# Second mixer's attention by pairs of heads instead of unit by unit, beside the dense matmuls of a two-block network

## The chip, the cores and the metric

One core of one Trainium2 chip runs the whole program. The metric is device time in microseconds (us) of one execution. The engines are TensorE (PE; its weight loads are listed as PEld), VectorE (DVE), ScalarE (ACT), GpSimd (POOL) and SyncE (SP, which issues the weight loads from memory). Each runs its own list of instructions in order and waits on semaphores.

## The reference, cut to what matters

Two network blocks run one after the other on 256 tokens of width 1024. The second has a feed-forward part, a mixer, and another feed-forward part. The mixer has two branches: a windowed attention (8 query heads of width 64 on 2 key/value heads, 16 meta tokens, a per-head distance bias, a sink logit) and a gated linear attention (4 heads). Each branch is multiplied by a weight matrix and a sigmoid gate, and the sum goes through w_out.

```python
s_band = jnp.einsum('bcqkgd,bcskd->bkgcqs', qf, kb).astype(jnp.float32) * scale
s_band = s_band - slopes[None, :, :, None, None, None] * dist[None, None, None]
s_meta = jnp.einsum('bcqkgd,bmkd->bkgcqm', qf, km).astype(jnp.float32) * scale
p = jax.nn.softmax(jnp.concatenate([s_meta, s_band, s_sink], axis=-1), axis=-1).astype(v.dtype)
of = (jnp.einsum('bkgcqm,bmkd->bcqkgd', p[..., :N_META], vm)
      + jnp.einsum('bkgcqs,bcskd->bcqkgd', p[..., N_META:N_META + NB], vb))
```

## The kernel before, in words

**Dense products.** Every float32 weight matrix is split on the chip into an upper part (ScalarE, `split`, L600, tile `hi`) and a lower part (DVE, `split`, L1128, tile `lo`), and every product is three matmuls: upper by upper, upper by lower, lower by upper (L1962 to L1964). Weights come through a ring of four slots (`raw`, `hi`, `lo`). A slot's weights feed one `half` of 24 matmuls of 256 columns. Results go to four accumulator banks `acc` in PSUM, two of them per pair of output tiles; `acc_free` says that a pair of banks has been read. Four more banks, `wk`, serve everything else.

**The stage.** The mixer's projections are the phase `in2k`. Its gates are `in2g`, 16 halves, of which four are done before the attention begins. `brb` (linear branch, four parts) and `bra` (attention branch, four parts) are the branch matrices, `wout2` is w_out. The attention (PE, L2608 to L2655) is laid between twelve halves of `in2g` and the four parts of `brb`, all listed by hand on each engine.

**A unit** is one head and one block of 128 queries: `UNITS` (L353) runs over head pairs `hp`, blocks `b` and the head `par` of the pair, 16 units. An early block (b = 0) sees 16 meta keys and 128 others (144 columns), a late one (b = 1) 272. The head of the pair sits in the upper or lower 64 partitions of `qT2`. Per step u, TensorE does:
- the scores of unit u (L2616), in bank u % 2, after the maximum of unit u - 1,
- for unit u - 2: a wait for its normalised probabilities, and their transposes by key tile into bank 2 (L2628, L2630),
- one dense piece of 24 matmuls,
- a wait for the transposes' copy, and the values (`transposed_out`, L2400) in bank 3. Here the value matrix `avz2` holds zeros on both sides of the 64 value columns, so a matmul of 128 columns adds one head's output to the one half of the partitions and zeros to the other; both heads of a pair accumulate in one group.

DVE has per step: the softmax sum and normalisation of unit u - 1 (`softmax_sum`, L1408 to L1410), the maximum with the bias added (L1878), the head pair's lower part (`heads_lower`, L1415), the lower part of a weight slot (`gates_split`), the evacuation of two gate tiles times the inverse norm (`gates_evac`, L1829), the output of a linear head (L1894 to L1897: reciprocal, product with the gain, product with the gate) in four of the steps, its lower part (L1902), and later `branch_out` (L1864), which reads a part of `brb` out of its bank. At the end come four products of gate and branch (L1912). ScalarE has per step: the copy of the transposes (L1066, L1067), the exponential and the sink's exponential (L766, L767), the upper part of a weight slot, the copy of a head pair (`heads_out`, L774), the copy of a linear head (L1080), and two sigmoids (L1058). GpSimd builds the bias of each head in a double buffer (L579).

**After it**, `evac_bra` on DVE (L1920, L1922, L1926) multiplies each part of `bra` by its gate, adds, and makes the lower part; ScalarE copies the upper part (L1089) and then splits the next weights. `wout2` starts when the third part has been read out of its bank.

**The first mixer** (L2187 to L2219) does its attention by pairs: `scores` puts two heads on two row halves, `values_out` two heads on two column halves.

```python
if 1 <= u <= 12:
    gates_half(u + 3)
elif 13 <= u <= 16:
    ...
    branch_part("brb", 4, u - 13)
elif u == 17:
    pe.wait_ge(ol_ready, 7)
    branch_part("bra", 0, 0, range(3))
```

Of the kernel before, what the change touches and what calls it, by code (L numbers as in the profile page):

```python
# [6 lines left out]
F32 = mybir.dt.float32  # L7
# [7 lines left out]
P = 128  # L15
# [97 lines left out]
def program(nc, dr, out):  # L113
    with ExitStack() as root:
# [146 lines left out]
        avz2 = sbuf(blk2, "avz2", [P, 3, 2, 192])  # L261
# [91 lines left out]
        UNITS = [(hp, b, par) for hp in range(4) for b in range(2) for par in range(2)]  # L353
# [124 lines left out]
        def _(pool):  # L478
# [93 lines left out]
            pool.memset(avz2[:], 0.0)  # L572
# [12 lines left out]
        def _(act):  # L585
# [183 lines left out]
            def heads_out(n, hp):  # L769

                if n == 0:
                    act.wait_ge(half_done, 4)
                act.wait_ge(o_ps, n + 1)
                act.activation(mixH[:, hp, :], wk[:, 3 if n >= 4 else 2, 0:T], ACT.Copy).then_inc(oh_ready, 1)  # L774
# [210 lines left out]
            def attention_keys():  # L985

                act.wait_ge(zero2, 1)
                act.wait_ge(av2_ps, 1)
                act.activation(avz2[0:META, 0, :, 64:128], wk[0:META, 2, 0:P].rearrange("p (g d) -> p g d", g=2), ACT.Copy)
                act.activation(avz2[:, 1:3, :, 64:128], wk[:, 2, P:3 * P].rearrange("p (t g d) -> p t g d", t=2, g=2),  # L990
# [70 lines left out]
            for u in range(18):  # L1061
                w = u - 2
                if w >= 0:
                    b = UNITS[w][1]
                    act.wait_ge(pt_ps, 16 + w + 1)
                    act.activation(pT2[0:META, w % 2, 0:P], wk[0:META, 2, 0:P], ACT.Copy)  # L1066
                    act.activation(pT2[:, w % 2, P:P * (b + 2)], wk[:, 2, P:P * (b + 2)], ACT.Copy).then_inc(pt_ready, 1)  # L1067
                if u < 16:
                    hp, b, par = UNITS[u]
                    nk = META + P * (b + 1)  # L1070
                    exp_scores(16 + u, Sm2[:, u % 2, 0:nk], sinkn[:, 8 + 2 * hp + par:9 + 2 * hp + par])

                gates_split(u + 6)
                if w >= 0 and w % 4 == 3:
                    heads_out(4 + w // 4, w // 4)
                if u in (3, 5, 7, 9):

                    n = u // 2 - 1
                    act.wait_ge(yb_ready, n + 1)
                    act.activation(mixH[:, 4 + HEADS[n], :], og[:, n, 0:T], ACT.Copy).then_inc(ybh_ready, 1)  # L1080
                if u == 16:
                    sigmoid(1)
            sigmoid(0)

# [1626 lines left out]
```

## Time and profile before

| | us |
|---|---|
| timed runs, median of 3 | 1023.13 (1020.88 to 1025.48) |
| the profiled execution's own time | 1014.95 |
| its span | 1013.2 |
| TensorE busy, share of the span | 977.3, 96% |
| DVE busy | 657.0, 65% |
| ScalarE busy | 498.4, 49% |
| GpSimd busy | 75.4, 7% |
| mean granted TensorE clock | 0.988 |

In the lines of the timeline the first number is an instruction's start, the second its duration (or that of a merged group of x instructions, from the first start to the last end), and in brackets stands the idle time of the engine before it, with what ended it. Durations on one engine overlap: a matmul is recorded for 0.28 us where the next one starts 0.12 after it. What an instruction takes of its engine's time is the distance of two starts. A float32 matmul shows as two records.

### The profile page before, as it was taken

How to read it: one execution, taken by the hardware profiler on the slowest of the kernel's cores; microseconds unless marked ns; L12 is line 12 of the kernel's file. 1: busy time of each engine (PE TensorE's matmuls, PEld its weight loads, DVE VectorE, ACT ScalarE, POOL GpSimd, SP SyncE). 2: the span in 40 equal slices, each digit the busy share in tenths (PEclk: the TensorE clock that was granted, in tenths of full speed). 3: DMA queues.
4: the chain of work that ended last, by engine and by line, in shares of the span. 5: the costliest groups of instructions: out<-in, count | busy, mean ns of one | idle time of the engine just before them, and what ended most of it. 6: DMA issues, size and time to landing. Idle time of an engine off the chain costs nothing.

```text
span 1013.2 us, 19459 instructions
## 1 busy us (share of the span) xinstructions
PE 977.3 (96%) x7547; PEld 910.4 (90%) x7547; DVE 657.0 (65%) x1008; ACT 498.4 (49%) x774; POOL 75.4 (7%) x101
## 2 busy tenths in 40 slices
PE   4998999999999999999999999999999999999996
PEld 2776777989999999899999999998888999999995
DVE  4788887577666765765555555754966775565553
ACT  3664546654545543554445334644545555444530
POOL 0102012110000021000000012000210100000000
PEclk8999998999999999999999999999999999999998
DMA  9953346456656794165556736542433556666841
GB/s 349 385 175 126 116 134 215 144 173 189 194 168 189 194 299 152 62 214 175 166 176 189 219 104 196 167 144 64 125 109 121 169 166 207 187 184 199 218 122 41
DMA packets 189439, 175.41 MB, mean 173 GB/s; under 512 B 7344, under 2 KB 178624, under 8 KB 189008
## 3 DMA queue, kind: packets, MB, share of 16 engines
q1 hardware_dynamic: 183888, 154.29, 49.8%
q0 software_dynamic: 4928, 17.51, 5.0%
q10 hardware_dynamic: 576, 2.97, 0.7%
q8 instruction: 31, 0.51, 0.2%
q14 instruction: 16, 0.13, 0.0%
HBM read 173.67 MB, written 1.05 MB: 172 GB/s over the span
## 4 chain that ended last, share of the span: by engine, by line
PE 86%; DVE 8%; ACT 3%; issue 2%; DMA 1%; SPq 0%; DVEq 0%; ACTq 0%
PE acc L1962 22%; PE acc L1963 22%; PE acc L1964 22%; PE acc L2348 2%; DVE lo L1128 2%; PE wk L2400 1%; PE acc L2152 1%; DMA slab_hi<-in_w_ada 1%; PE acc L2153 1%; PE acc L2154 1%; ACT hi L600 1%; DVE inv L1182 1%; PE wk L2616 1%; PE wk L1962 1%; PE wk L1964 1%
## 5 line engine op out<-in xcount | busy, mean ns | idle before, releaser
L1128 DVE TENSOR_TENSOR lo<-raw,hi 128x1024 fp32r<-128x1024 f32 (+1 forms) x260 | 333.7, 1296 | 199.9 <-ACT hi L600 199.5
L600 ACT ACTIVATE hi<-raw 128x1024 fp32r<-128x1024 f32 (+1 forms) x260 | 282.9, 1098 | 132.2 <-PE acc L1964 123.7
L1962 PE MATMUL acc<-nH,hi 128*128 128x272 f32 (+3 forms) x1016 | 291.2, 287 | 2.9 <-DVE gab L1920 1.1
L1963 PE MATMUL acc<-nL,hi 128*128 128x272 f32 (+3 forms) x1016 | 289.7, 285 | 0.0
L1964 PE MATMUL acc<-nH,lo 128*128 128x272 f32 (+3 forms) x1016 | 288.7, 284 | 0.0
L1962 PEld LDWEIGHTS acc<-nH,hi 128*128 128x128 f32 (+1 forms) x1016 | 191.4, 188 | 5.4 <-DVE lo L1128 2.1
L1963 PEld LDWEIGHTS acc<-nL,hi 128*128 128x128 f32 (+1 forms) x1016 | 191.0, 188 | 0.4
L1964 PEld LDWEIGHTS acc<-nH,lo 128*128 128x128 f32 (+1 forms) x1016 | 190.9, 188 | 0.2
L1962 PE MATMUL acc<-gH,hi 128*128 128x256 f32 (+1 forms) x528 | 149.5, 283 | 0.8 <-DVE lo L1128 0.8
L1964 PE MATMUL acc<-gH,lo 128*128 128x256 f32 (+1 forms) x528 | 149.2, 283 | 0.0
L1963 PE MATMUL acc<-gL,hi 128*128 128x256 f32 (+1 forms) x528 | 149.0, 282 | 0.0
L1962 PE MATMUL acc<-mixH,hi 128*128 128x256 f32 x400 | 113.9, 285 | 0.9 <-DVE mixL L1415 0.9
L1963 PE MATMUL acc<-mixL,hi 128*128 128x256 f32 x400 | 113.2, 283 | 0.0
L1964 PE MATMUL acc<-mixH,lo 128*128 128x256 f32 x400 | 113.1, 283 | 0.0
L1962 PEld LDWEIGHTS acc<-gH,hi 128*128 128x128 f32 x528 | 99.1, 188 | 1.0 <-DVE lo L1128 1.0
L1963 PEld LDWEIGHTS acc<-gL,hi 128*128 128x128 f32 x528 | 99.6, 189 | 0.0
L1964 PEld LDWEIGHTS acc<-gH,lo 128*128 128x128 f32 x528 | 99.2, 188 | 0.0
L1962 PEld LDWEIGHTS acc<-mixH,hi 128*128 128x128 f32 x400 | 76.7, 192 | 1.1 <-DVE mixL L1415 1.1
L1963 PEld LDWEIGHTS acc<-mixL,hi 128*128 128x128 f32 x400 | 76.8, 192 | 0.0
L1964 PEld LDWEIGHTS acc<-mixH,lo 128*128 128x128 f32 x400 | 76.7, 192 | 0.0
L544 POOL TENSOR_TENSOR sq<-sq 128x256 f32<-128x256 f32 (+1 forms) x28 | 24.5, 876 | 497.4 <-ACT sq L890 442.5
L890 ACT ACTIVATE sq<-R (+3 forms) x36 | 15.8, 440 | 57.8 <-DVE R L1702 49.7
(421 smaller groups left out, 1307.9 us busy)
## 6 DMA issues: line engine op xcount, KB each, us to landing
raw<-in_w_in SPq DMA_DIRECT2D x52, 512.0 KB, 3.6
raw<-in_w_ffn_in SPq DMA_DIRECT2D x44, 512.0 KB, 4.4
raw<-in_ffn_w_gate SPq DMA_DIRECT2D x44, 512.0 KB, 3.6
raw<-in_ffn_w_up SPq DMA_DIRECT2D x44, 512.0 KB, 3.6
raw<-in_ffn_w_down SPq DMA_DIRECT2D x32, 704.0 KB, 4.8
stage<-in_w_ada POOLq DMA_DIRECT2D x24, 512.0 KB, 5.5
raw<-in_w_ffn_out SPq DMA_DIRECT2D x16, 704.0 KB, 6.5
raw<-in_w_out SPq DMA_DIRECT2D x16, 512.0 KB, 3.4
```

Of the source, the lines that this page charges most:

```text
L544: ins = pool.tensor_tensor(sq[:, 0, 0:width], sq[:, 0, 0:width], sq[:, k, 0:width], ALU.add)
L600: act.activation(hi[:, j, 0:width], raw[:, j, 0:width], ACT.Copy).then_inc(hi_ready, 1)
L890: act.activation(sq[:, k, 0:width], R[:, k, t0:t0 + width], ACT.Square).then_inc(sq_ready, 1)
L1128: dve.tensor_tensor(lo[:, j, 0:width], raw[:, j, 0:width], hi[:, j, 0:width].bitcast(F32), ALU.subtract).then_inc(lo_ready, 1)
L1182: link(dve.reciprocal(inv[:, 0:width], rms[:, 0:width]))
L1962: pe.matmul(out_, wH, xH, start=start, stop=False)
L1963: pe.matmul(out_, wH, xL, start=False, stop=False)
L1964: return pe.matmul(out_, wL, xH, start=False, stop=stop)
L2152: pe.matmul(out_, n5H[:, k, rows], hi[:, k // 2, w], start=k == 0, stop=False)
L2153: pe.matmul(out_, n5H[:, k, rows], lo[:, k // 2, w], start=False, stop=False)
L2154: return pe.matmul(out_, n5L[:, k, rows], hi[:, k // 2, w], start=False, stop=k == KD - 1)
L2348: ins = pe.matmul(out_, ws[:, j, w], xs[:, k, :], start=k == 0 and m == 0 and n == 0, stop=k == KD - 1 and n == 2, skip_group_check=True)
```

## The change

The step by units becomes a loop over eight pairs n (head pair n // 2, block n % 2), on each of the three engines.

- TensorE, per pair: both heads' scores one after the other on the two row halves, in banks 0 and 1; the values of the pair before, on two column halves, from `av2`, which holds the 128 value columns without zeros; a dense piece; the transposes of both heads, into the banks that held their scores; a second dense piece. The first values wait for the linear heads' root means. After the loop: the last values, three quarters of `bra`'s first part, a wait for the last heads' lower part, and the rest.
- Head pairs alternate between banks 2 and 3 (`head_bank`).
- ScalarE, per pair: two exponentials, the heads' copy (n = 2, 4, 6), a split, one copy of both heads' transposes (two instructions of twice the width), a split, a linear head's copy (n = 0, 1, 3, 4). Then: sigmoid, the last heads' copy, split 22, sigmoid, split 23.
- DVE, per pair: two maxima, two softmax sums, heads' lower part, a split, a gate evacuation, a linear head's output (n = 0, 1, 3, 4), a split, a linear lower part (n = 1, 2, 4, 5); brb's parts are read out in pairs 6 and 7. Then: the last heads' lower part, split 22, the last part of brb, the four products, split 23.
- GpSimd no longer clears the value matrix, and ScalarE doesn't wait for it.

```diff
-        avz2 = sbuf(blk2, "avz2", [P, 3, 2, 192])
+        av2 = sbuf(blk2, "av2", [P, 3, P])
...
+        LINEAR_AT = {0: 0, 1: 1, 3: 2, 4: 3}
+        def head_bank(n):
+            return wk[:, 2 + n % 2 if n >= 4 else 2 + n // 4, 0:T]
...
-            pool.memset(avz2[:], 0.0)
...
+            for n in range(8):
+                hp, b = divmod(n, 2)
+                for par in range(2):
+                    exp_scores(16 + 2 * n + par, Sm2[:, par, 0:keys_to(b)], sinkn[:, 8 + 2 * hp + par:9 + 2 * hp + par])
+                if n >= 2 and b == 0:
+                    heads_out(4 + hp - 1, hp - 1)
+                gates_split(6 + 2 * n)
+                act.wait_ge(pt_ps, 16 + 2 * n + 2)
+                act.activation(pT2[0:META, :, 0:P], wk[0:META, 0:2, 0:P], ACT.Copy)
+                act.activation(pT2[:, :, P:P * (b + 2)], wk[:, 0:2, P:P * (b + 2)], ACT.Copy).then_inc(pt_ready, 2)
+                gates_split(7 + 2 * n)
+                if n in LINEAR_AT:
+                    i = LINEAR_AT[n]
+                    act.wait_ge(yb_ready, i + 1)
+                    act.activation(mixH[:, 4 + HEADS[i], :], og[:, i, 0:T], ACT.Copy).then_inc(ybh_ready, 1)
+            sigmoid(1)
+            heads_out(7, 3)
+            gates_split(22)
             sigmoid(0)
+            gates_split(23)
...
+            for n in range(8):
+                hp, b = divmod(n, 2)
+                shifted_maxima(n)
+                for par in range(2):
+                    softmax_sum(16 + 2 * n + par, Sm2[:, par, 0:keys_to(b)])
+                if n >= 2 and b == 0:
+                    heads_lower(4 + hp - 1, hp - 1)
+                if n == 7:
+                    branch_out(1)
+                gates_split(6 + 2 * n)
+                if n <= 6:
+                    gates_evac(n + 1)
+                if n in LINEAR_AT:
+                    linear_out(LINEAR_AT[n])
+                gates_split(7 + 2 * n)
+                if n - 1 in LINEAR_AT:
+                    linear_lower(LINEAR_AT[n - 1])
+                if n == 6:
+                    branch_out(0)
+                if n == 7:
+                    branch_out(2)
+            heads_lower(7, 3)
+            gates_split(22)
+            branch_out(3)
+            dve.wait_ge(gates_ready, 1)
+            dve.wait_ge(acc_free[1], USE["brb"] + 2)
+            for j in range(4):
+                b = gab[:, KD + 2 * j:KD + 2 * j + 2, :]
+                dve.tensor_tensor(b, b, branch[j], ALU.mult)
+            gates_split(23)
...
+            def paired_values(n):
+                hp, b = divmod(n, 2)
+                pe.wait_ge(pt_ready, 16 + 2 * n + 2)
+                if n == 0:
+                    pe.wait_ge(grms, 2)
+                if b == 0 and hp >= 2:
+                    pe.wait_ge(ol_ready, 4 + hp - 1)
+                g4 = hp // 2
+                for t in range(b + 2):
+                    rows = slice(0, META if t == 0 else P)
+                    for par in range(2):
+                        ins = pe.matmul(wk[HD * par:HD * par + HD, 2 + hp % 2, P * b:P * b + P],
+                                        av2[rows, t, HD * g4:HD * g4 + HD], pT2[rows, par, P * t:P * t + P],
+                                        start=t == 0, stop=t == b + 1)
+                if b == 1:
+                    ins.then_inc(o_ps, 1)
...
+            for n in range(8):
+                paired_scores(n)
+                if n >= 1:
+                    paired_values(n - 1)
+                mixer_piece(2 * n)
+                paired_probabilities(n)
+                mixer_piece(2 * n + 1)
+            paired_values(7)
+            pe.wait_ge(ol_ready, 7)
+            branch_part("bra", 0, 0, range(3))
```

`paired_scores(n)` waits for the copy of pair n - 1's transposes, then issues the two score matmuls. `paired_probabilities(n)` waits for each head's normalised probabilities before its transposes. `mixer_piece(i)` is a half of `in2g` for i < 12 and a part of `brb` after that, as before.

## Rows read from the trace of the kernel before

**Rows 1.** The page, section 4: the chain that ended last, by engine.
```profile
PE 86%; DVE 8%; ACT 3%; issue 2%; DMA 1%; SPq 0%; DVEq 0%; ACTq 0%
```

**Rows 2.** Windows: length, busy us (instructions) by engine, granted clock, DMA share, GB/s.
```profile
700.60:789.20 88.60, 86.56 (x633) 76.49 (x633) 66.51 (x142) 49.28 (x115) 13.08 (x6) 1.00 0.35 114
...
710.00:715.00 5.00, 5.00 (x40) 4.48 (x39) 4.83 (x15) 2.73 (x8) 2.48 (x1) 1.00 0.35 104
```

**Rows 3.** Timeline, TensorE: a late block's values, scores, transposes, between dense matmuls.
```profile
716.76 0.28 PE L1964 MATMUL acc<-nH,lo 128*128 128x256 f32 x1
716.97 1.12 PE L2400 MATMUL wk<-pT,avz 16*128 16x128 f32 x6
718.02 0.51 PE L2616 MATMUL wk<-kS,qT 64*128 64x144 f32 x2
718.46 0.28 PE L2628 MATMUL wk<-cst,Sm 128*16 128x128 f32 x1
...
718.91 0.29 PE L1963 MATMUL acc<-nL,hi 128*128 128x256 f32 x1
719.03 0.28 PE L1964 MATMUL acc<-nH,lo 128*128 128x256 f32 x1
```

**Rows 4.** Timeline, TensorE: an early block's values and a late block's scores.
```profile
726.57 0.90 PE L2400 MATMUL wk<-pT,avz 16*128 16x128 f32 x4
727.40 0.72 PE L2616 MATMUL wk<-kS,qT 64*128 64x272 f32 x2
728.05 0.28 PE L2628 MATMUL wk<-cst,Sm 128*16 128x128 f32 x1
```

**Rows 5.** Timeline, TensorE: paired scores and values in the first mixer.
```profile
114.30 0.59 PE L2195 MATMUL wk<-kTs,qT 64*128 64x512 f32 x1
114.30 0.59 PE L2195 MATMUL wk<-kT,qT 64*128 64x512 f32 x1
114.82 1.09 PE L2217 MATMUL wk<-pT,vat 128*64 128x128 f32 x16
115.85 0.50 PE L2152 MATMUL acc<-hi,n5H 128*128 128x512 f32 x1
```

**Rows 6.** Timeline, DVE: linear output, sum, maximum, split, evacuation.
```profile
708.16 1.74 DVE L1894 RECIPROCAL tC<-tC 128x256 f32<-128x256 f32 x1
...
710.81 0.15 DVE L1408 TENSOR_TENSOR rinv<-rsum,esink 128x1 f32<-128x1 f32 x1
...
711.47 0.49 DVE L1878 CUSTOM_DVE_ANT_0 Sm<-wk,bias,sinkn 128x272 f32<-128x272 f32 x1
...
711.89 1.22 DVE L1128 TENSOR_TENSOR lo<-raw,hi 128x1024 fp32r<-128x1024 f32 x1
713.02 0.68 DVE L1829 TENSOR_TENSOR gab<-acc,inv 128x512 f32<-128x512 f32 x1
713.62 0.15 DVE L1408 TENSOR_TENSOR rinv<-rsum,esink 128x1 f32<-128x1 f32 x1
```

**Rows 7.** Timeline, ScalarE: exponential with sink, then the split.
```profile
712.00 0.52 ACT L766 ACTIVATE Sm<-Sm,negm 128x272 f32<-128x272 f32 x1 [1.85 <-DVE negm L1878]
...
712.71 1.04 ACT L600 ACTIVATE hi<-raw 128x1024 fp32r<-128x1024 f32 x1
```

**Rows 8.** Timeline: ScalarE's table load and sigmoid, bra's first evacuation, wout2's first matmul.
```profile
771.62 1.28 ACT L1058 ACT_TABLE_LOAD   x1
...
774.73 0.25 ACT L1066 ACTIVATE pT<-wk 16x128 f32<-16x128 f32 x1
...
779.86 0.69 DVE L1920 TENSOR_TENSOR gab<-gab,acc 128x512 f32<-128x512 f32 x1 [0.32 <-ACT gab L1058]
...
789.20 0.36 PE L1962 MATMUL acc<-nH,hi 128*128 128x256 f32 x1 [1.11 <-DVE gab L1920]
```

**Rows 9.** Timeline, TensorE: transposes in the first mixer after a wait.
```profile
97.53 1.15 PE L2203 MATMUL wk<-cst,Sm 128*128 128x128 f32 x7 [2.91 <-DVE Sm L1436]
```

**Rows 10.** Windows, columns as in rows 2: what follows that wait.
```profile
98.60:102.00 3.40, 3.40 (x10) 2.70 (x9) 3.33 (x10) 0.82 (x2) 0.00 (x0) 0.50 0.00 0
```

More of the change, by code:

```diff
@@ L773, in heads_out @@
                 act.wait_ge(o_ps, n + 1)
[L774 removed]
+                act.activation(mixH[:, hp, :], head_bank(n), ACT.Copy).then_inc(oh_ready, 1)
             def state_weights(h):
@@ L1898, in _, with linear_out @@
-                if u in (4, 6, 8, 10):
-                    n = u // 2 - 2
-                    dve.wait_ge(ybh_ready, n + 1)
-                    dve.tensor_tensor(mixL[:, 4 + HEADS[n], :], og[:, n, 0:T], mixH[:, 4 + HEADS[n], :].bitcast(F32),
-                                      ALU.subtract).then_inc(ybl_ready, 1)
-                if 14 <= u <= 17:
-                    branch_out(u - 14)
-                if u == 17:
-                    dve.wait_ge(gates_ready, 1)
-                    dve.wait_ge(acc_free[1], USE["brb"] + 2)
-                    for j in range(4):
-                        b = gab[:, KD + 2 * j:KD + 2 * j + 2, :]
-                        dve.tensor_tensor(b, b, branch[j], ALU.mult)
+            def linear_out(n):
+                root = (tC, kdT)[n // 2][:, n % 2, 0:T]
+                dve.wait_ge(gr_ready, 2)
+                dve.wait_ge(grms, n // 2 + 1)
+                link(dve.reciprocal(root, root))
+                link(dve.scalar_tensor_tensor(out=og[:, n, 0:T], in0=og[:, n, 0:T], scalar=col(V_GO), in1=root,
+                                              op0=ALU.mult, op1=ALU.mult))
+                dve.tensor_tensor(og[:, n, 0:T], og[:, n, 0:T], grT[:, HEADS[n], :], ALU.mult).then_inc(yb_ready, 1)
@@ L2394, in _ @@
                     ada_turn(3)
-            def transposed_out(par, b, keys):
-                for i, (v, p) in enumerate(keys):
-                    ins = pe.matmul(wk[:, 3, P * b:P * b + P], v, p, start=par == 0 and i == 0,
-                                    stop=par == 1 and i == len(keys) - 1)
-                if b == 1 and par == 1:
-                    ins.then_inc(o_ps, 1)
             PACED = [(k, s) for k in range(6) for s in range(2)] + [(6, 0), (7, 0), (6, 1), (7, 1)]
@@ new lines, in paired_scores, with paired_probabilities @@
+            def paired_scores(n):
+                hp, b = divmod(n, 2)
+                if n >= 1:
+                    pe.wait_ge(pt_ready, 16 + 2 * n)
+                for par in range(2):
+                    h = 2 * hp + par
+                    keys = kvraw2[:, 0, :] if h // 4 == par else kS2
+                    pe.matmul(wk[:, par, 0:keys_to(b)], qT2[lanes(h), hp, P * b:P * b + P], keys[lanes(h), 0:keys_to(b)],
+                              start=True, stop=True).then_inc(s_ps, 1)
+            def paired_probabilities(n):
+                for par in range(2):
+                    pe.wait_ge(p_norm, 16 + 2 * n + par + 1)
+                    ins = pe.transpose(wk[0:META, par, 0:P], Sm2[:, par, 0:META], ident)
+                    for t in range(n % 2 + 1):
+                        ins = pe.transpose(wk[:, par, P + P * t:2 * P + P * t], Sm2[:, par, META + P * t:META + P * t + P], ident)
+                    ins.then_inc(pt_ps, 1)
@@ new lines, in mixer_piece @@
+            def mixer_piece(i):
+                if i < 12:
+                    gates_half(4 + i)
+                else:
+                    if i == 12:
+                        pe.wait_ge(ybl_ready, 4)
+                    branch_part("brb", 4, i - 12)
+            for n in range(8):
+                paired_scores(n)
+                if n >= 1:
+                    paired_values(n - 1)
+                mixer_piece(2 * n)
+                paired_probabilities(n)
+                mixer_piece(2 * n + 1)
```

102 lines of the change are left out of this document (15 added, 87 removed).

## The prediction

> **What bounds the kernel now.** First the page: the chain that ended last is TensorE for 86% [rows 1], so only what shortens TensorE's own sequence, or a wait in it, moves the end. Then the windows over the stretch that the change touches, from the first scores of the second mixer's attention at 700.6 to the first matmul of the phase wout2 at 789.2 [rows 2]: TensorE is busy 86.56 of 88.60 us, so about 2 us of it are waits. VectorE (DVE) is busy 66.51 us there, but 4.83 of 5.00 in a window where the linear heads' output is worked on: it has spare time in total and almost none in the first half. Then TensorE's timeline, read from start to start, since durations overlap.
>
> **What a unit costs now** [rows 3, 4]. Dense matmuls start 0.12 apart. From the last dense one to the values is 0.21, so a change of the array's shape costs 0.09 beyond the pitch. Values of a late block (three key tiles) take 718.02 - 716.97 = 1.05; of an early block (two) 727.40 - 726.57 = 0.83. Scores take 718.46 - 718.02 = 0.44 and 728.05 - 727.40 = 0.65. Three transposes and one dense matmul take 718.91 - 718.46 = 0.45, so three transposes 0.33, two 0.22. A dense piece is 24 matmuls, 2.87.
>
> **The change on TensorE, part by part.**
> *Scores.* Two heads of a pair go out together on different row halves. The first mixer does this already: its two streams start in the same hundredth [rows 5]. So a pair costs one price, 0.44 or 0.65. For 16 units I count 8.7 now (4.4 after): the first two already run together, so 3.9 saved, and the entries fall from 16 x 0.09 to 9 x 0.09, another 0.6; I keep 4.2 for both, since the last two units enter no scores now.
> *Values.* The compact matrix has 64 columns per head and the two heads go side by side. No row of before shows 16 rows by 64 columns. Lower end: the first mixer's 128x64 pairs, 16 records from 114.82 to 115.85 [rows 5], 0.26 per key tile, so 0.52 early and 0.77 late. Upper end: the pair doesn't overlap and costs two units, 1.66 and 2.10. I take 0.68 and 0.90, the lower end plus 0.15 for the shape change between the 16-row and the 128-row tile, because rows 5 have the same two column halves in the same program. That is 15.0 now against 6.3: 8.7 saved.
> The Trainium skill (TensorEngine Tiling, Key Properties) says that changing the tiling mode, not just the tile, drains the engine; it speaks against this change, which has four mode changes per pair, but it gives no price, and by the 0.09 to 0.15 taken here the sum stands.
> *Transposes and dense pieces* keep their number. TensorE's work falls by 12.9 us in all. The bank moves (heads in turn in two banks, transposes in the score banks), the smaller matrix, and the dropped memset and wait on GpSimd cost nothing: the keys are copied while dense matmuls of the projections run.
>
> **What takes part of it back: the order on DVE.** DVE prices [rows 6]: maximum 0.42, softmax sum 0.66, split 1.13, evacuation 0.60, a linear head's output 710.81 - 708.16 = 2.65. ScalarE's exponential with the sink 712.71 - 712.00 = 0.71 [rows 7]. An early block has 144 columns for 272; I estimate its maximum, sum and exponential at 0.35, 0.60 and 0.60. Now a maximum waits for scores issued a whole unit before, and there is always one unit in hand. After, a pair is one serial chain: scores, two maxima, two exponentials, two sums, transposes. From the first maximum to the second sum's end: 0.5 + 2 x 0.71 + 0.1 + 0.75 = 2.8 late, 2.5 early. TensorE covers it with the previous values and one piece, 0.68 + 2.87 = 3.55 or more; enough, if DVE is free when the scores land.
> Between the second sum and the next maxima DVE has split, evacuation, linear output, split, and about 0.3 waiting for ScalarE's split (1.04, begun when DVE's sum of 0.7 begins): 0.3 + 1.13 + 0.60 + 2.65 + 1.13 = 5.8, and 0.35 more for each lower half. Pair 0 to 1: 5.8 + 2.8 + 0.1 = 8.8 from one second sum to the start of the next second transposes, against TensorE's 0.14 to start again after a wait, second transposes 0.22, piece 2.87, entry and scores 0.74, values 0.68, piece 2.87, first transposes 0.33 = 7.9: a wait of 0.9. Pair 1 to 2: 6.1 + 2.5 + 0.1 = 8.7 against 7.9: 0.8. Pair 2 to 3 has no linear output: none. Pair 3 to 4 lives on the lead that DVE gained: none. Pair 4 to 5: 6.5 + 2.8 + 0.1 = 9.4 against 7.8 and some 0.3 of lead: 1.2. Pair 0 starts behind an activation table load: 0.55. In pair 6 the second dense piece (brb's second part) needs the bank freed by DVE's last gate evacuation, which stands behind the sums, a lower half and a split: 0.35 + 0.3 + 1.13 + 0.68 + 0.14 = 2.6 after the second sum, less the lead of 1.2 that the sum has by then and the transposes' 0.44: 1.0. Sum of waits 4.5.
> So the second transposes of the last pair start at 700.6 + 15 pieces 43.0 + entries 0.7 + scores 4.4 + values 5.4 (seven) + transposes 4.2 + waits 4.5 = 762.7.
>
> **The tail.** The end of the stage is now no longer TensorE's. In the bra phase each part goes evacuate, add, ScalarE copy, ScalarE split, DVE split, evacuate; the first evacuation at 779.86 leads to wout2's first matmul at 789.20, 9.34 us [rows 8], and that chain is unchanged. After, the first evacuation comes at the end of this: transposes land 0.5, pair copy out of PSUM 0.9 (twice as wide as now; bounds 0.4 and 0.9, I take the high one), ScalarE split 0.95, table load and sigmoid 774.73 - 771.62 = 3.1 [rows 8], copy of the last heads 0.3 to its start of the next, split 22 1.05; then on DVE, in its new order, split 1.14, last brb evacuation 0.60, four gate products at 0.60 (the 128x512 shape of [rows 6]), split 23 1.14: 5.3. Together 12.1: 774.8. Before, the sigmoid stood a unit earlier and the gate products ran before the last heads. TensorE meanwhile waits for bra's second bank about 1.5 (last brb evacuation at 770.9, behind the last heads' lower half and split 22), and about 1.3 at each of bra's third and fourth parts and at wout2. wout2 then starts at 774.8 + 9.3 = 784.1, against 789.20: **5.1 us gained**. Check: 12.9 less work, 10.2 of waits against 2.3 now.
>
> The profiled execution took 1014.95 (span 1013.2 and 1.75 around it); less 5.1 that is 1009.9. The three timed runs have a median of 1023.13, 8.2 above the profiled one, and spread 4.6. The sum is a difference, so I put it on the median: 1018.0. A measurement of this kernel can tell about 0.5%, 5.1 us, from no change; the forecast sits on that line.
>
> **Rivals.**
> A. *DVE's waits don't show.* If DVE's lead carries it through the linear heads, the 4.5 of waits go and wout2 starts 4.5 earlier: gain 9.6, 1013.5. For: DVE has 22 us idle [rows 2]. Against: 4.83 of 5.00 just where its order is tightest. 0.13.
> B. *Pairs of values don't overlap in the 16-row form,* or not at all. Seven values at the upper end add 7.5 to TensorE before the last transposes, of which half falls into the waits above: gain 1.3, 1021.8. Against: rows 5. 0.08.
> C. *The clock.* After 2.91 us without a matmul [rows 9] the granted clock was 0.50 over 98.6 to 102.0 [rows 10], the 1.2 GHz level, for 3.4 us. The tail after has four waits of 1.3 to 1.5 within 17 us where before has one or two; a stretch at the low level loses up to 1.7 us of dense matmuls, two on end 3.4, part of it inside waits: gain 2 to 3.5, 1020.4. The Trainium skill (TensorE: Matmul & The Clock Gate, What's actually happening) says that the gate follows how busy the engine has been recently, and by that rule this rival would hold. Against: waits of 1.1 at the end of this stage now left the clock at 1.00 [rows 2]. 0.15.
> D. *Slower: ScalarE late for the exponentials.* In its queue the next pair's exponentials stand behind the pair copy, the second split and the linear copy (0.9 + 0.95 + 0.35 = 2.2 after the transposes). I have about 1.4 of slack before the maxima need it. If the transposes' waits push this past zero, every pair is longer by up to 1.4: eight pairs 11.2, slower by 6.1, 1029.2. It decides from 0.64 us per pair. For: ScalarE waits 1.85 now only because DVE is late. Against: it is busy 49 of 89 us [rows 2]. 0.09.
>
> **How the numbers follow.** The forecast case has 0.55; its own spread of 1.5 either way puts half above the 0.5% line. Faster: A and half the forecast, and a little of C, 0.43. Slower by over 0.5%: D, mostly, 0.07. Within: 0.50. Range: forecast, A, C and B, 1013.2 to 1023.4.
>
> **What would show it.** Right: score records in pairs starting together; values of both heads started within 0.01 and 0.7 to 0.9 per pair; DVE's maxima late in pairs 1, 2 and 5 and TensorE waiting there for the softmax sum; waits of over 1 us before bra's second, third and fourth part; wout2 starting some 83.5 us after the first scores. Wrong: values over 1.5 a pair, a clock under 1.00 between 700 and 785, no TensorE waits in the tail, or a stretch over 88 us.

## The result, and the profile after

| | before | after |
|---|---|---|
| median of ten runs, us | 1022.0 (1015.72 to 1025.62) | 1013.85 (1011.02 to 1019.19) |
| profiled execution, us | 1014.95 | 1015.63 |
| its span, us | 1013.2 | 1013.8 |
| TensorE busy in the span | 977.3 (96%) | 975.2 (96%) |

The ratio of the times is 0.9934, interval 0.9909 to 0.9959: faster, by less than 1%, and the forecast's range holds the time, 0.65 us above its lower end. A second measurement of the same two kernels, further down, gives 0.9957, interval 0.9927 to 0.9987.

The two profiled executions alone would say "no change". That is the first thing to take apart. The changed kernel's scores begin at 706.01, before's at 700.6 [rows 2]; wout2 begins at 789.87 against 789.20; from there to the end both take 223.9 to 224.0. So the stretch fell from 88.62 (first scores to wout2's first matmul, by the records) to 83.86, 4.8 us, and the code ahead of it, where the change drops only the clearing of the value matrix and a wait for it, took 5.4 us longer in this one execution. The experiments return to that.

The page's chain by engine, after:

```profile
PE 81%; DVE 11%; ACT 4%; issue 3%; DMA 1%; SPq 0%; DVEq 0%; ACTq 0%
```

TensorE's share fell from 86% [rows 1] and VectorE's (DVE's) rose from 8% to 11%: work went, waits on VectorE came. The windows over the stretch, with the columns of rows 2, and over two pieces before it:

```profile
706.01:789.87 83.86, 76.52 (x634) 67.89 (x633) 66.67 (x142) 46.88 (x99) 9.61 (x6) 1.00 0.38 120
20.00:30.00 10.00, 8.49 (x34) 6.63 (x31) 6.64 (x17) 6.22 (x12) 0.00 (x0) 1.00 1.06 370
680.00:690.00 10.00, 10.00 (x53) 8.38 (x51) 6.53 (x15) 5.03 (x6) 0.00 (x0) 0.83 0.33 105
```

TensorE is busy 76.52 where it was busy 86.56 [rows 2]: 10.0 less. It idles 83.86 - 76.52 = 7.3 where it idled 2.0. That is 10.0 saved and 5.3 given back. The granted clock is 1.00 in the stretch, but 0.83 in the ten microseconds from 680.

TensorE's timeline where the scores of a late pair (272 columns) and the values of the early pair before it stand, then the values of that late pair:

```profile
713.22 0.49 PE L2623 MATMUL wk<-kvraw,qT 64*128 64x272 f32 x1
713.22 0.49 PE L2623 MATMUL wk<-kS,qT 64*128 64x272 f32 x1
...
713.88 0.80 PE L2647 MATMUL wk<-pT,av 16*64 16x128 f32 x8
714.61 0.39 PE L1977 MATMUL acc<-nH,hi 128*128 128x256 f32 x1
714.84 0.28 PE L1978 MATMUL acc<-nL,hi 128*128 128x256 f32 x1
...
722.61 1.02 PE L2647 MATMUL wk<-pT,av 16*64 16x128 f32 x12
...
723.56 0.39 PE L1977 MATMUL acc<-nH,hi 128*128 128x256 f32 x1
```

Scores of the two heads start in the same hundredth, and the pair takes 713.88 - 713.22 = 0.66, what one head took [rows 4]. Values of two heads take 714.61 - 713.88 = 0.73 and 723.56 - 722.61 = 0.95, where one head took 0.83 and 1.05 [rows 3, 4]. Behind the values, the first dense matmul takes 714.84 - 714.61 = 0.23 instead of 0.12. The summary of TensorE's waits between 700 and 800:

```profile
PE acc L1977 <- DVE gab L1935: 3.5, 3, 1.3
PE wk L2630 <- DVE Sm L1413: 2.1, 6, 0.6
PE acc L1977 <- DVE kdT L1867: 1.3, 1, 1.3
PE acc L1977 <- DVE gab L1832: 0.4, 1, 0.4
```

Each line has total, number and longest. The first and third are the tail: bra's banks and wout2 wait for VectorE. The second is the loop: the softmax sums of pairs 0, 1, 2 and 5. The fourth is pair 6, which waits for a gate evacuation. The tail, on ScalarE:

```profile
769.55 1.04 ACT L607 ACTIVATE hi<-raw 128x1024 fp32r<-128x1024 f32 x1
770.61 1.28 ACT L1064 ACT_TABLE_LOAD   x1
771.90 1.92 ACT L1064 ACTIVATE gab<-gab 128x2048 f32<-128x2048 f32 x1
773.72 0.36 ACT L781 ACTIVATE mixH<-wk 128x256 fp32r<-128x256 f32 x1
```

and on VectorE:

```profile
774.12 0.42 DVE L1418 TENSOR_TENSOR mixL<-wk,mixH 128x256 fp32r<-128x256 f32 x1 [1.67 <-ACT mixH L781]
775.06 1.22 DVE L1131 TENSOR_TENSOR lo<-raw,hi 128x1024 fp32r<-128x1024 f32 x1 [0.52 <-ACT hi L607]
776.20 0.68 DVE L1867 COPY kdT<-acc 128x512 f32<-128x512 f32 x1
776.99 0.69 DVE L1926 TENSOR_TENSOR gab<-gab,tA 128x512 f32<-128x512 f32 x1
...
778.81 0.68 DVE L1926 TENSOR_TENSOR gab<-gab,kdT 128x512 f32<-128x512 f32 x1
779.41 1.22 DVE L1131 TENSOR_TENSOR lo<-raw,hi 128x1024 fp32r<-128x1024 f32 x1
780.54 0.68 DVE L1935 TENSOR_TENSOR gab<-gab,acc 128x512 f32<-128x512 f32 x1
```

and on TensorE:

```profile
776.94 0.39 PE L1977 MATMUL acc<-mixH,hi 128*128 128x256 f32 x1 [1.30 <-DVE kdT L1867]
781.28 0.38 PE L1977 MATMUL acc<-mixH,hi 128*128 128x256 f32 x1 [1.21 <-DVE gab L1935]
785.47 0.39 PE L1977 MATMUL acc<-mixH,hi 128*128 128x256 f32 x1 [1.07 <-DVE gab L1935]
789.87 0.36 PE L1977 MATMUL acc<-nH,hi 128*128 128x256 f32 x1 [1.26 <-DVE gab L1935]
```

The last heads' lower half waits 1.67 for ScalarE, whose copy stands behind a table load and a sigmoid; then VectorE works without a gap through split, copy, four products and another split, up to bra's first evacuation at 780.54, and TensorE waits four times for what comes out.

### The profile page after: what moved, and what is told of

Read it like the earlier page. It is cut to its first block, busy times and chain, and to the rows that moved or that the text cites. A ratio compares the mean times of both kernels' runs of the same rounds, so it can differ in the third digit from the quotient of the medians.

```text
span 1013.8 us, 19425 instructions
## 1 busy us (share of the span) xinstructions
PE 975.2 (96%) x7547; PEld 907.4 (89%) x7547; DVE 657.4 (65%) x1008; ACT 496.1 (49%) x758; POOL 71.7 (7%) x100
## 3 DMA queue, kind: packets, MB, share of 16 engines
HBM read 173.67 MB, written 1.05 MB: 172 GB/s over the span
## 4 chain that ended last, share of the span: by engine, by line
PE 81%; DVE 11%; ACT 4%; issue 3%; DMA 1%; SPq 0%; DVEq 0%; ACTq 0%
PE acc L1977 21%; PE acc L1978 21%; PE acc L1979 21%; DVE lo L1131 2%; PE acc L2363 2%; ACT hi L607 1%; PE acc L2167 1%; PE acc L2168 1%; PE acc L2169 1%; DMA raw<-in_w_ada 1%; PE wk L2036 1%; DVE inv L1185 1%; PE wk L1977 1%; PE wk L2218 1%; PE wk L1979 1%
```

## The experiments

In all of them "the stretch" is the time from the first scores to wout2's first matmul. It is read from the trace, holds the whole of the change, and leaves out what differs from run to run ahead of it. The time from wout2 to the end was 223.7 to 224.1 in every trace.

### Before and after, once more

The same two kernels, without an edit.

> The kernel before again, for a second trace of it: a stretch of 88.6. If the short stretch at half clock at about 683 us, which all traces but the first of before show, comes with the change, it is absent here; if it is chance, it may be here too, and the stage then begins at 703 to 707 instead of 700.6.

> The changed kernel itself, unchanged, beside the others of this call on one chip. The stretch from the first scores to wout2 should be 83.9 again, and the ratio to the kernel before 0.993 to 0.995 (4.8 us of 1019). What varies is the time at which the stage begins (700.6 in the trace of before, 703.8 to 706.9 in five others): if stretches of half clock before it are chance, this run may show another start.

Measured: before 88.61, changed 83.84. The windows of the two stretches, before first:

```profile
701.31:789.92 88.61, 86.57 (x633) 76.50 (x633) 66.53 (x142) 49.26 (x115) 13.08 (x6) 1.00 0.38 114
```

```profile
704.01:787.86 83.85, 76.54 (x634) 67.88 (x633) 66.68 (x142) 46.88 (x99) 9.61 (x6) 1.00 0.39 120
```

Both repeat to 0.02 us. The gain in the stretch is 88.61 - 83.84 = 4.8 us. The times: 1016.16 (12 runs) against 1021.03 (20 runs), ratio 0.9957, interval 0.9927 to 0.9987.

The single times fall into clusters. Here they stand beside the mean granted clock that each run shows. Two clusters of each kernel have the same mean clock, so the clock alone doesn't tell those two apart; they are matched by their order.

```
mean clock      before, us             changed, us
0.988 / 0.989   1015.74 to 1015.96     1011.18 to 1011.59
0.988 / 0.989   1020.53 to 1021.51     1016.07, 1016.26
0.985 / 0.986   1018.44, 1018.48       1013.58, 1014.86
0.984 / 0.983   1025.25 to 1025.68     1020.96, 1021.06
0.981-3 / 0.980 1021.74 to 1023.90     1018.50 to 1019.11
```

Cluster by cluster the changed kernel is lower by 4.5 (1015.9 to 1011.4), 4.8 (1021.0 to 1016.2), 4.2 and 4.5 us (by the clusters' middles), and about 4 in the last row, where the clocks differ a little: about the stretch's gain of 4.8 each time. In the first measurement six of the ten runs of the changed kernel lay between 1013.25 and 1014.28 and only two above 1018, while six of before's ten lay above 1020. The stretch's 4.8 of 1022.0 is a ratio of 0.9953; that the first measurement gives 0.9934 is put down here to that mixture, by these counts.

### Values one head after the other

The changed loop, but with the zero-padded matrix and 128 columns per head again, a pair's two heads one after the other:

```diff
...
-                for t in range(b + 2):
-                    rows = slice(0, META if t == 0 else P)
-                    for par in range(2):
-                        ins = pe.matmul(wk[HD * par:HD * par + HD, 2 + hp % 2, P * b:P * b + P],
-                                        av2[rows, t, HD * g4:HD * g4 + HD], pT2[rows, par, P * t:P * t + P],
-                                        start=t == 0, stop=t == b + 1)
+                for par in range(2):
+                    vs = slice(64, 192) if par == 0 else slice(0, P)
+                    for t in range(b + 2):
+                        rows = slice(0, META if t == 0 else P)
+                        ins = pe.matmul(wk[:, 2 + hp % 2, P * b:P * b + P], avz2[rows, t, g4, vs],
+                                        pT2[rows, par, P * t:P * t + P], start=par == 0 and t == 0,
+                                        stop=par == 1 and t == b + 1)
```

> The stretch is the time from the first scores of the second mixer to the first matmul of wout2: 88.6 us before the change, 83.9 after it. Here the loop by pairs stays and the values go back to the 128-column matrix with zeros, one head after the other. By my account (TensorE's work less, DVE's order takes part back) a pair's values go from 0.73 and 0.95 to about 1.7 and 2.1, 8 us more work on TensorE, of which more than half falls into the waits for the softmax sums and before bra: a stretch of 87.4. Rival, that TensorE's work is the whole account: 83.9 + 8 = 92. Rival, that the values did not matter and the paired scores gave the gain: 84 to 85.

Measured: stretch 86.82 (703.84 to 790.66), one time of 1016.45. The waits:

```profile
PE acc L1979 <- DVE gab L1937: 3.5, 3, 1.3
PE acc L1979 <- DVE kdT L1869: 0.4, 1, 0.4
PE wk L2632 <- DVE Sm L1415: 0.2, 1, 0.2
```

So pairing the scores and reordering the loop gives 88.61 - 86.82 = 1.8, and the values on two narrow column halves, side by side, give another 3.0. The longer values stand where the waits for the softmax sums were: those fall from 2.1 to 0.2, and the wait in pair 6 is gone. A pair's values take 1.49 and 1.94 here, 0.73 and 0.95 in the change, 7.0 us less over the eight pairs; 3.0 of it stay and 4.0 are absorbed by waits.

### Before's order with the compact matrix

Before's sixteen units, each with one column half of the compact matrix in place of 128 columns with zeros:

```diff
...
-                    ins = pe.matmul(wk[:, 3, P * b:P * b + P], v, p, start=par == 0 and i == 0,
-                                    stop=par == 1 and i == len(keys) - 1)
+                    ins = pe.matmul(wk[HD * par:HD * par + HD, 3, P * b:P * b + P], v, p, start=i == 0,
+                                    stop=i == len(keys) - 1)
...
```

> The kernel before, unit by unit, with the compact matrix alone: each unit's values are 64 columns wide on one column half, with nothing beside them. If the gain comes from two heads side by side, a unit costs what a pair costs in the changed kernel less nothing, 0.73 and 0.95 for 0.83 and 1.05 before, so 16 x 0.1 = 1.5 us less: a stretch of 87.3. If narrow weights alone gave the gain (half the columns, half the price), a unit would cost about 0.45 and 0.6, and the stretch would be 82 to 83.

Measured: stretch 86.99 (706.10 to 793.10), one time of 1018.85. TensorE at an early unit:

```profile
713.14 0.28 PE L1962 MATMUL acc<-nH,lo 128*128 128x256 f32 x1
713.35 0.79 PE L2398 MATMUL wk<-pT,av 16*64 16x128 f32 x4
714.07 0.49 PE L2614 MATMUL wk<-kS,qT 64*128 64x272 f32 x1
```

One head's values take 714.07 - 713.35 = 0.72. A pair's take 0.73. The second head is free.

The compact matrix alone saves 1.6 of the stretch, with no pairing at all: 0.11 in each of the 14 units whose values stand in front of scores. The last two units have transposes behind their values. There before, and this kernel, show

```profile
768.86 0.90 PE L2400 MATMUL wk<-pT,avz 16*128 16x128 f32 x4
769.60 0.27 PE L2628 MATMUL wk<-cst,Sm 128*16 128x128 f32 x1
```

```profile
772.91 0.79 PE L2398 MATMUL wk<-pT,av 16*64 16x128 f32 x4
773.63 0.28 PE L2626 MATMUL wk<-cst,Sm 128*16 128x128 f32 x1
```

0.74 against 0.72 (and 0.96 against 0.94 for the late unit). So the width of the weights is worth only 0.02 a unit. The other 0.09 of before's 0.83 is the step from a 128-column values matmul to the 64-row scores, and the compact form takes 0.72 in front of either. 14 x 0.11 and 2 x 0.02 are 1.6. The kernel above fits this: its two wide heads, with no scores behind them, take 1.49, twice 0.74 or so.

### No linear output on VectorE

The change as it is, without the reciprocal and the gain product of the linear heads' output, so that the linear branch isn't normalised:

```diff
-                link(dve.reciprocal(root, root))
-                link(dve.scalar_tensor_tensor(out=og[:, n, 0:T], in0=og[:, n, 0:T], scalar=col(V_GO), in1=root,
-                                              op0=ALU.mult, op1=ALU.mult))
```

> The changed kernel, with the reciprocal and the gain product left out of each linear head's output (2.3 of 2.65 us of DVE, four times; so the linear branch isn't normalised). If these are what makes the maxima late, the waits for the softmax sums in pairs 1, 2 and 5 go (2.7 us of them) and the stretch is 81.1. If ScalarE's queue or the chain of the softmax itself makes them, the waits stay and the stretch is 83.9.

Measured: stretch 81.09 (705.16 to 786.25), one time of 1012.05. The waits:

```profile
PE acc L1974 <- DVE gab L1932: 3.5, 3, 1.3
PE acc L1974 <- DVE kdT L1867: 1.3, 1, 1.3
PE acc L1974 <- DVE gab L1832: 0.4, 1, 0.4
PE wk L2627 <- DVE Sm L1413: 0.2, 1, 0.2
```

Only the wait for the softmax sums changed, 2.1 to 0.2, and the stretch fell by 2.8 (the 0.46 idle in pair 1 is 0.63 from start to start). So those waits come from the linear outputs that stand between two pairs on VectorE, and not from the softmax itself or from ScalarE. ScalarE's own records agree: in the changed kernel it sat idle for 1.01 to 3.18 us before the first exponential of pairs 1 to 7, each time for VectorE's maximum. The tail and pair 6 are untouched by it.

### The first key tile padded to 128 rows

The changed kernel with the two operands zeroed once, and the metadata tile run over all 128 rows:

```diff
...
-                    rows = slice(0, META if t == 0 else P)
+                    rows = slice(0, P)
```

> The changed kernel, with the first key tile of the values matmul widened from its 16 rows (the metadata keys) to all 128: the other 112 rows of weights and values are zeroed once and add nothing. The values pairs then no longer go from a 16-row matmul to 128-row matmuls. If that step between shapes is what a values pair costs beyond its records, a pair falls from 0.73 us (early) and 0.95 us (late) by 0.10 to 0.15 us, to about 0.60 and 0.82; most of it goes into longer waits for the softmax sums of pairs 0, 1, 2 and 5, so the stretch from the first scores to the second output product's first matmul goes only from 83.85 to 83.3 to 83.8. Rival: the 16-row matmul costs what any other does, a values pair stays at 0.73 and 0.95 within 0.03, and the stretch stays at 83.85.

Measured: stretch 83.65 (706.55 to 790.20), one time of 1015.99. The values of the same early and late pair:

```profile
714.41 0.66 PE L2650 MATMUL wk<-pT,av 128*64 128x128 f32 x8
715.00 0.39 PE L1980 MATMUL acc<-nH,hi 128*128 128x256 f32 x1
...
723.11 0.88 PE L2650 MATMUL wk<-pT,av 128*64 128x128 f32 x12
723.91 0.39 PE L1980 MATMUL acc<-nH,hi 128*128 128x256 f32 x1
```

0.59 and 0.80, against 0.73 and 0.95: the step from 16 rows to 128 rows inside a pair costs 0.14 to 0.15. Seven of the eight pairs save 1.0 together (the last takes 0.99 in both kernels), but the waits for the sums grow from 2.1 to 2.7 and that in pair 6 from 0.4 to 0.6, and the stretch keeps 0.2 of it. Of 1.0 us less work for TensorE in this loop, 0.2 reached the end.

### Orders of the tail

Three kernels take the tail apart, and a fourth the wait in pair 6. The first has two edits: on ScalarE the last branch's sigmoid moves ahead of the last pair's split and copy; on VectorE the gate products and the evacuations of brb that don't need the last heads move ahead of their lower half.

```diff
+                if n == 7:
+                    sigmoid(1)
...
-            sigmoid(1)
             heads_out(7, 3)
...
+            def gated(j):
+
+                dve.wait_ge(acc_free[j % 2], USE["brb"] + j // 2 + 1)
+                b = gab[:, KD + 2 * j:KD + 2 * j + 2, :]
+                dve.tensor_tensor(b, b, branch[j], ALU.mult)
...
                 if n == 7:
                     branch_out(1)
+                    dve.wait_ge(gates_ready, 1)
+                    gated(0)
+                    gated(1)
                 gates_split(6 + 2 * n)
+                if n == 7:
+                    branch_out(2)
+                    gated(2)
...
-                if n == 7:
-                    branch_out(2)
+            branch_out(3)
             heads_lower(7, 3)
+            gated(3)
             gates_split(22)
-            branch_out(3)
-            dve.wait_ge(gates_ready, 1)
-            dve.wait_ge(acc_free[1], USE["brb"] + 2)
-            for j in range(4):
-                dve.tensor_tensor(b, b, branch[j], ALU.mult)
             gates_split(23)
```

> The changed kernel, with the last heads' sigmoid ahead of the last pair's transposes on ScalarE, and on DVE brb's parts and their gate products as soon as they are there, before the last heads' lower part. If the tail is bound by that order, the first evacuation of bra comes 2.2 us earlier and the stretch is 81.5, 0.2% of the whole time. If it is bound by something that the order doesn't touch (the arrival of bra's weights, the heads' copy), the stretch stays at 83.9.

Measured: stretch 81.53 (706.90 to 788.43), 2.3 less. The time was 1016.39 against 1019.0 for before, ratio 0.9952, interval 0.9922 to 0.9983; its profiled execution had 10 us more at half clock between 693.3 and 703.6.

The second has the ScalarE edit alone:

> The changed kernel with one edit on ScalarE: the last branch's sigmoid stands before the last pair's split and its transposes' copy, VectorE's order stays. Together with the VectorE order it gave 81.5 us, with the VectorE order alone 85.8 us in a trace that also held a half-clock stretch inside. If the two only help together, the sigmoid alone gives 0.6 us: 83.2 us. Rival: ScalarE is what the tail waits for, and the sigmoid alone gives nearly all of it, 81.5 to 82.

Measured: 83.08 (705.30 to 788.38), one time of 1014.11. That is 0.8 of the 2.3.

The third has the VectorE edit alone, and was run twice:

> The DVE order of e4_tail_order without the earlier sigmoid on ScalarE. DVE then stops at its first gate product until the sigmoid is done, with split 20 behind it, which bra's first part needs: TensorE waits about 4.5 us there, and the stretch is 85.6, longer than the changed kernel's 83.9. Rival, that the products' place alone makes the tail: 81.5 to 83.

> VectorE's tail order without the earlier sigmoid, again, since the earlier look had a half-clock stretch inside the tail (771.0 to 777.8). VectorE then waits 4.4 us for the branch's factor. If that wait sets the end, the stretch is again within 0.5 us of 85.8 with or without a half-clock stretch. Rival: the half-clock stretch made it, and without one the stretch is 83 to 84 us.

Measured: 85.78 (700.65 to 786.44), with one time of 1012.19, and 85.75 (708.62 to 794.37), with one of 1020.32. VectorE in the first of them:

```profile
761.70 0.69 DVE L1867 COPY tB<-acc 128x512 f32<-128x512 f32 x1
768.48 0.69 DVE L1874 TENSOR_TENSOR gab<-gab,tA 128x512 f32<-128x512 f32 x1 [6.09 <-ACT gab L1064]
```

and TensorE behind it:

```profile
771.61 0.55 PE L1983 MATMUL acc<-mixH,hi 128*128 128x256 f32 x1 [4.40 <-DVE tC L1867]
```

The product is moved ahead, its factor is not: VectorE idles 6.09 and all that is queued behind it is late, TensorE by 4.40. The half of an order that gives 2.3 loses 1.9 alone. Both traces also have the clock low for 6.8 us inside the stretch, at 771.0 to 777.8 in one and at 777.5 to 784.4 in the other, which is 70.4 and 68.9 after the first scores. So the repeat doesn't show the order without a low clock. What shows that the clock doesn't make the 1.9 is VectorE: from the first product at 768.48 to bra's first evacuation at 777.10 it has no idle time, and the same from 776.44 to 785.05 in the second trace. TensorE worked for 6.2 us at the low clock in one and 4.8 in the other, and the stretches agree to 0.03.

The fourth has only the evacuation that pair 6 waits for, moved ahead of a split:

```diff
+                if n == 6:
+                    gates_evac(7)
                 gates_split(6 + 2 * n)
-                if n <= 6:
+                if n <= 5:
                     gates_evac(n + 1)
```

> The changed kernel with one edit on VectorE: the evacuation that pair 6 waits for stands before the split of mixed tokens instead of behind it. If the 0.7 us wait of TensorE in pair 6 is that evacuation's place in VectorE's order, it goes, and with it up to 1.0 us of the stretch: 82.9 us, against 83.85. Rival: pair 6 waits next for its softmax sums, which the evacuation pushes back, and the stretch stays within 0.2 us of 83.85.

Measured: 83.14 (705.28 to 788.42), one time of 1014.2. The wait of 0.4 for `gab` L1832 is gone from the waits and the others are unchanged. 0.7 of the 1.0 at most came.

### All orders together

The tail's two edits, the evacuation's, and one more on ScalarE: in the bra phase the split of the next weights ahead of the copy of the mixed tokens.

```diff
-            pipeline("bra", 1024, evac_bra, K4, True, behind=((0,), (1,), (), (2, 3)))
+            for j in range(4):
+                if j < 2:
+                    split(BASE["wout2"], j, 1024)
+                evac_bra(0, j)
+            for q in (2, 3):
+                split(BASE["wout2"], q, 1024)
```

> The changed kernel with three orders changed: the tail as in e4_tail_order, the last gate evacuation on DVE ahead of the split in pair 6, and in the bra phase ScalarE's split of the next weights ahead of its copy of the mixed tokens. By the price sums: 81.5, less 1.0 for the evacuation, less 2.6 because DVE's split no longer waits for a copy that waits for DVE: a stretch of 77.9, 6 us less than the changed kernel and 10.7 less than before, a ratio of 0.988 to 0.990. Rival, that each wait removed comes back as another one: 80 or more.

Measured: stretch 78.24 (703.62 to 781.86), 5.6 less than the change and 10.4 less than before. Time 1010.3 against 1021.03, ratio 0.9907, interval 0.9874 to 0.9939. The waits that are left:

```profile
PE wk L2644 <- DVE Sm L1419: 2.1, 6, 0.6
PE acc L1991 <- DVE mixL L1424: 0.4, 1, 0.4
PE acc L1991 <- issue: 0.2, 1, 0.2
```

All four tail waits of the changed kernel are gone. By difference, 5.6 - 2.3 - 0.7 leaves 2.6 for the edit in the bra phase, which no kernel has alone. It is the fastest of the kernels timed here; its cluster at 0.985 is 1007.4, against before's 1018.5 at the same clock: 11 us.

### What set the beginning of the stretch

The code ahead of the first scores is the same in all of these kernels, but for the clearing and the copy of the value matrix. The half-clock stretches recorded ahead of them are not:

```
kernel               low stretches before the first scores, us in all    first scores
before (second)      17.0                                                701.31
VectorE order        17.1                                                700.65
changed (second)     23.8                                                704.01
short linear         27.3                                                705.16
VectorE order (2nd)  34.1                                                708.62
```

These are five of the fourteen traces; the second one of before starts its first mixer's scores at 66.48, the others of the table at 65.7 to 65.9, and that is its extra 0.7. From 17 to 34 us at half clock the scores move by 8.0, some 0.47 us for each. The first profile of the changed kernel has 17.0 recorded and begins at 706.01 all the same. Its missing stretch is at the start, where the page's clock is 1.00 (the window 20 to 30, above) and the matmuls say otherwise. Its TensorE timeline, then the window from 20 to 30 of the changed kernel's second trace:

```profile
28.95 0.41 PE L2100 MATMUL acc<-n5H,hi 128*128 128x256 f32 x1
29.16 0.41 PE L2100 MATMUL acc<-n5L,hi 128*128 128x256 f32 x1
29.38 0.41 PE L2100 MATMUL acc<-n5H,lo 128*128 128x256 f32 x1
```

```profile
20.00:30.00 10.00, 7.43 (x33) 6.50 (x33) 8.78 (x21) 5.73 (x11) 0.00 (x0) 0.66 1.06 370
```

These start 0.21 apart, where the same shape starts 0.12 apart at full clock: TensorE ran at the lower level, 1.2 GHz, until about 31 us, with nothing recorded. Inside the recorded low stretch of the VectorE-order kernel, 771.0 to 777.8, they start 0.21 apart too. Its first mixer's scores come 2.2 us later (68.0 against 65.7). Two other traces, the compact-matrix and the full-rows kernel, also show 1.00 there, matmuls 0.21 apart until about 31, and first scores at 68.07 and 68.39. Two later half-clock stretches that before lacks, 110.0 to 113.4 and 683.4 to 686.9, are 6.9 us; at 0.47 each they give an estimated 3.2, the rest.

The stretch near 680 to 687 stands in eight of the fourteen traces of this case, and is missing in both of before, in the second one of the changed kernel, in both with the VectorE order and in the full-rows one. The compact-matrix kernel, which keeps before's order of units, has it. So the pairing isn't needed for it and doesn't bring it with every execution; whether the change makes it more frequent stays open. So does what sets it.

## Why the prediction was right

**Step by step.** The forecast put the stretch at 83.5 and it came to 83.86 and 83.84. From the first scores to the last pair's second transposes it said 62.1; the trace has 768.26 - 706.01 = 62.25. That these agree so well is partly luck, as the terms show. To bra's first evacuation it said 74.2; the trace has 74.5. From there to wout2 it said 9.3 and 9.33 was measured.

**The terms.** Scores, 0.44 and 0.65 a pair: right, both heads start together. Values, taken at 0.68 and 0.90: mis-sized by 0.05, measured 0.73 and 0.95. The lower end plus a price for the shape change was the right construction. The padded experiment shows the step at 0.14 to 0.15 where 0.15 had been taken; but by that experiment the bare lower end is 0.59 and 0.80, not 0.52 and 0.77. Two tiles at 0.59 and three at 0.80 are 0.21 a tile and 0.17 for the pair as a whole; four tiles by the same numbers are 1.01, against the first mixer's 1.03 [rows 5]. The forecast had divided a fixed part by four tiles and multiplied it by two or three. One term was left at nothing: in the new order dense matmuls follow the values, and the first of them takes 0.22 to 0.23 instead of 0.12 (714.61 to 714.84 above). That is 0.10 a pair, 0.7 us up to the last pair's transposes, beside 0.4 for the values.

The Trainium skill (TensorEngine Tiling, Key Properties) says that a change of tiling mode drains the engine. The 0.14 to 0.15 inside a pair is in line with it, if the 16-row and the 128-row tile count as two modes, and has a size here: 8 pairs times 0.15 is 1.2 us of TensorE, a tenth of what the change removes.

**The waits.** They were forecast in pairs 0, 1, 2 and 5 for the softmax sum and in pair 6 for the evacuation, and they stand there and nowhere else. Counted from start to start they are 0.52, 1.02, 0.43 and 1.28 in pairs 0, 1, 2 and 5, where 0.55, 0.9, 0.8 and 1.2 were forecast. The one in pair 6 was put at 1.0 and is 760.51 - 759.80, less one step of 0.12, so 0.6. Together 3.8, not 4.5: the 0.7 too much here made good most of the 1.1 too little in the terms. That the linear output is their cause was an argument in the forecast; the short-linear kernel shows it. That the table load, sigmoid and VectorE's order make bra's first evacuation late was another; the tail experiments show it for 2.3 us, and that neither edit brings this alone.

**The profiled work.** The profile's 10.0 less and 5.3 more count busy time up to a matmul's modelled end. The forecast's 12.9 less work and 10.2 of waits count from start to start, restarts included. Counted so, the trace has 9.3 of waits (3.8 in the loop, 5.5 in the tail) against 2.3 before, and so 11.8 less work. Both were forecast about 1 us too large, and the two errors cancel: 5.0 forecast, 4.8 measured. The 1.1 of work is the values' 0.05 and the 0.10 behind them, eight times.

**The rivals.** A, no waits: excluded by the waits; what it would have brought is what the short-linear kernel shows, 2.8 rather than 4.5, because pair 6's wait and a part of pair 0's have other causes and stay. B, values not overlapping: excluded; with its two heads one after the other a pair took 1.49 and 1.94, under the upper end of 1.66 and 2.10, whose 0.83 and 1.05 hold the step to the scores, and a gain of 1.8 was left where the rival said 1.3. C, the clock: at 1.00 through the stretch in both traces of the change, with dense matmuls 0.12 apart. It can happen: TensorE's wait of 4.40 in the VectorE-order kernel ends at 771.61, and the clock is low from 771.0. It cost nothing that can be seen there, 85.78 against the 85.6 expected without it, as VectorE worked on without a gap. D, ScalarE late: no wait of TensorE on ScalarE's exponentials in any trace, removing VectorE work alone took the loop's waits away, and ScalarE waited 1.01 to 3.18 us for VectorE before the exponentials of pairs 1 to 7.

**The number.** 1018.0 was 4.2 above the median. 1.1 us of it is the median of before, 1023.13 from three runs and 1022.0 from ten. The sum, 5.1 against 4.8, goes the other way by 0.3. The remaining 3.4 are put down to which clusters the ten runs of the changed kernel fell into: in the second measurement the median was 1016.16. That 1013.85 still lay inside the range, 0.65 above its end, is luck as much as forecast, since the range was built from the rivals and has no term for the clusters, which lie 2.5 to 5 us apart. "On the line of 0.5%" was a fair description: 4.8 of 1020 is 0.47%, and both intervals hold the line of 0.995.

## What to carry to other kernels

Pairing small matmuls on row and column halves gives the second head for nothing, but where the dense pieces between the pairs cover a serial chain, the other engines' order decides how much of it stays: here 10.0 us of TensorE work bought 4.8. After such a change look for the next wait at once: reorderings alone, with no work removed, brought 5.6 more. Move a consumer ahead only together with the producer of its operand; the consumer's half of the move alone cost 1.9. And price a small matmul together with what stands behind it: the same two key tiles took 0.83 in front of scores and 0.74 in front of transposes.

## What was not expected of the hardware

- The page's granted clock can be 1.00 while TensorE runs at its lower level: 128x256 matmuls 0.21 apart instead of 0.12 up to 31 us in three traces. The pitch of equal matmuls is the safer sign.
- Half-clock stretches of 3.4 to 13.7 us stand at other places in executions of the same code, also where TensorE shows no wait (683.4 to 686.9, busy 10.00 of 10.00). The Trainium skill (TensorE: Matmul & The Clock Gate, What's actually happening) lets the gate follow how busy the engine has been; that is in line with the stretch that begins within a wait of 4.40, and it doesn't by itself explain these.
- The values of one head on one column half (0.72) take as long as those of two heads on both (0.73). With 128 columns of weights one head takes 0.74, and 0.83 where 64-row scores follow.
- Stretches equal to 0.03 us between executions stand beside whole times that differ by 8 us (1012.19 and 1020.32, the two with the VectorE order): in the traces, what varies is where TensorE's clock is low ahead of the stretch, 17.1 and 34.1 us in these two.
